# Gate and up products of a hierarchical mixture of experts: from fp32 to three fp32r products, with the weights split block by block on ScalarE and VectorE

## The reference

```
t = rms_norm(x, norm2_gain)
g_prob = softmax(t @ w_group + b_group); g = top 1 of g_prob
e_logit = t @ w_router + b_router;      2 best experts inside group g
gates = softmax(of the two logits) * p(g)
hg = einsum('td,edf->tef', t, w_gate)       # D = 1024, f = 256
hu = einsum('td,edf->tef', t, w_up)
a = silu(hg) * hu * gates
x = x + einsum('tef,efd->td', a, w_down)
```

## Time and profile before

| | |
|---|---|
| median of 3 runs | 1723.99 us (1722.34 to 1726.35) |
| the profiled execution, its own time | 1723.27 us |
| its span in the profile | 1721.4 us |
| PE busy | 1491.7 us (87%) |
| DVE busy | 781.1 us (45%) |
| ACT busy | 452.3 us (26%) |
| POOL busy | 315.3 us (18%) |
| DMA | 221.09 MB, mean 128 GB/s |

### The profile page before, as it was taken

How to read it: one execution, slowest core, us unless ns; L and a number is a source line. 1 busy time by engine, 2 the same in 40 slices (tenths; PEclk the granted TensorE clock), 3 DMA queues, 4 the chain that set the end, 5 groups by cost and what they waited for, 6 DMA issues and landing times.

```text
span 1721.4 us, 22556 instructions
## 1 busy us (share of the span) xinstructions
PE 1491.7 (87%) x6963; PEld 1079.8 (63%) x6964; DVE 781.1 (45%) x1883; ACT 452.3 (26%) x886; POOL 315.3 (18%) x204
## 2 busy tenths in 40 slices
PE   5999978998992999999289998899999749999990
PEld 4878867886882444444178786788778624444440
DVE  5777656663336122212267866656533452212210
ACT  4231245662111011111222222567412101111110
POOL 1000068001000122222500001930200012222224
PEclk9999989999995999999599999899999869999995
DMA  8000020000168499973870002000002945999947
GB/s 314 19 1 0 0 98 1 2 1 1 73 222 291 156 283 298 341 223 89 226 222 0 1 0 98 1 1 2 1 25 90 330 154 160 270 301 280 311 91 162
DMA packets 116624, 221.09 MB, mean 128 GB/s; under 512 B 5976, under 2 KB 72736, under 8 KB 116544
## 3 DMA queue, kind: packets, MB, share of 16 engines
q1 hardware_dynamic: 91744, 131.82, 22.2%
q0 software_dynamic: 19136, 69.38, 16.4%
q10 hardware_dynamic: 5664, 18.88, 2.8%
HBM read 170.77 MB, written 49.28 MB: 128 GB/s over the span
## 4 chain that ended last, share of the span: by engine, by line
PE 77%; DVE 7%; issue 6%; DMA 3%; ACT 2%; POOL 1%; ACTq 1%; DVEq 0%; PEld 0%; PEldq 0%; POOLq 0%; SPq 0%
PE ps L1566 19%; PE ps L1360 17%; PE ps L1340 11%; PE ps L1493 9%; PE ps L1579 9%; PE ps L1446 7%; PE ps L1420 2%; DMA out_x<-x_res,arena 2%; PE ps L1507 2%; PE ps L1422 1%; POOL out_x L622 1%; DVE arena L1149 1%; PE ps L1480 1%; DVE w_in_lo L944 1%; DMA big<-in_w_in 1%
## 5 line engine op out<-in xcount | busy, mean ns | idle before, releaser
L1566 PE MATMUL ps<-big,arena 128*128 x720 | 325.8, 606 | 9.6 <-issue 8.3
L1340 PE MATMUL ps<-cst,arena 128*128 128x128 f32 x1242 | 186.4, 284 | 76.4 <-DVE arena L915 37.6
L905 DVE TENSOR_TENSOR arena<-ps,par 128x512 f32<-128x512 f32 x126 | 81.2, 686 | 355.8 <-PE ps L1340 355.8
L1566 PEld LDWEIGHTS ps<-big,arena 128*128 128x128 f32 x720 | 135.7, 194 | 170.4 <-issue 170.4
L1340 PEld LDWEIGHTS ps<-cst,arena 128*128 128x128 f32 x1242 | 152.6, 146 | 122.7 <-DVE arena L915 39.3
L1360 PE MATMUL ps<-w_in_hi,hT_hi 128*128 128x512 f32 x512 | 206.1, 402 | 12.7 <-DVE hT_lo L933 9.9
L1360 PE MATMUL ps<-w_in_hi,hT_lo 128*128 128x512 f32 x512 | 202.1, 395 | 0.0
L1360 PE MATMUL ps<-w_in_lo,hT_hi 128*128 128x512 f32 x512 | 201.9, 394 | 0.0
L614 POOL DMA_INDIRECT x_res<-token_rows,row_tok x62 | 61.0, 985 | 605.1 <-issue 309.2
L1579 PE MATMUL ps<-big,arena 128*128 x360 | 163.8, 598 | 5.4 <-issue 5.4
L1446 PE MATMUL ps<-big,arena 128*128 128x64 f32 x1152 | 149.7, 278 | 0.0
(11 more groups left out here) (169 smaller groups left out, 1770.1 us busy)
## 6 DMA issues: line engine op xcount, KB each, us to landing
big<-in_w_gate SPq DMA_DIRECT2D x32, 1024.0 KB, 10.6
big<-in_w_up SPq DMA_DIRECT2D x32, 1024.0 KB, 13.1
big<-in_w_down SPq DMA_DIRECT2D x32, 1024.0 KB, 15.3
big<-in_w_in SPq DMA_DIRECT2D x16, 1024.0 KB, 9.5
big<-in_w_out SPq DMA_DIRECT2D x4, 2048.0 KB, 10.3
token_rows<-arena ACTq DMA_DIRECT2D x16, 512.0 KB, 3.3
out_x<-x_res ACTq DMA_DIRECT2D x16, 512.0 KB, 4.1
x_res<-out_x SPq DMA_DIRECT2D x8, 512.0 KB, 5.8
```

The source lines that it names most:

```text
L905: ins = ve.tensor_tensor(out=dst[:, 4 * h:4 * h + 4, :], in0=ps[:, banks + h, :].rearrange("p (a c) -> p a c", c=P), in1=spread(gain[:, 4 ...
L1340: ins = te.transpose(ps[:, bank + i // 4, (i % 4) * P:(i % 4 + 1) * P], src, ident)
L1566: ins = te.matmul(ps[:, 2, :], xgT[:, k, :], big[:, ds(at + k * 2 * FE, 2 * FE)], start=k == 0, stop=k == K - 1)
```

## The change

1. **Products.** `gate_up` takes 24 fp32r matmuls of 512 columns in place of 8 in fp32.
2. **Splitting the rows.** ACT copies the transposed rows of a block from PSUM into `xgT_hi` (`rows_high`, 128 x 1024) and DVE writes the rest into `xgT_lo` (`rows_evac`, 128 x 1024).
3. **Splitting the weights.** For every block, and again where two blocks share an expert, the gate and up weights are split in two halves of 128 x 2048: `gu_high` on ACT, `gu_low` on DVE. There are three buffers of a half, and half (t, h) goes to buffer (2t + h) mod 3. Each call looks up the block's expert in `block_e` with a register load from SBUF.
4. **Order.** In step t, ACT and DVE have, in this order:

```diff
+        xgT_hi = nc.alloc_sbuf_tensor_at("xgT_hi", [P, D], f32r, offset=xr_start)[:, :].rearrange("p (k n) -> p k n", n=P)
+        xgT_lo = nc.alloc_sbuf_tensor_at("xgT_lo", [P, D], f32r, offset=xr_start + 4 * D)[:, :].rearrange("p (k n) -> p k n", n=P)
+        HALF_GU = K * 2 * FE // 2
+        gu_hi = [part(f"gu_hi{i}", at, HALF_GU) for i, at in enumerate((0, 2 * HALF_GU, AT_A))]
+        gu_lo = [part(f"gu_lo{i}", at + HALF_GU, HALF_GU) for i, at in enumerate((0, 2 * HALF_GU, AT_A))]
...
+                def load_gu(e):
+                    slot = slot_of(e)
+                    for w, c in ((w_gate, 0), (w_up, K * FE)):
+                        sp.dma_start(w_gu[slot][:, c:c + K * FE],
+                                     w.rearrange("l e (p k) f -> p (l e) (k f)", k=K)[:, ds(l * NE + e, 1), :]
+                                     .rearrange("p a f -> p (a f)")).then_inc(s_gu[slot], 16)
...
+                for e in range(SLOTS, NE + 2):
+                    if e < NE:
+
+                        ended = sp.value_load(start_i[0:1, e - SLOTS + 1:e - SLOTS + 2], min_val=0, max_val=BLOCKS)
+                        sp.wait_ge(gu_split, upto(l, 2 * BLOCKS, 2 * ended))
+                        sp.sem_inc(s_passed, 1)
+                        load_gu(e)
+                    if SLOTS < e <= NE:
+                        report_gu(e - 1)
+                    d = e - 2
+                    if d >= SLOTS:
+                        ended = sp.value_load(start_i[0:1, d - SLOTS + 1:d - SLOTS + 2], min_val=0, max_val=BLOCKS)
                         sp.wait_ge(dn_done, upto(l, BLOCKS, ended))
...
+                        load_dn(d)
+                        if d > SLOTS:
+                            report_dn(d - 1)
...
-                in_high(l + 1, 0)
-
+                def gu_high(t, slot, h, half_of=None):
+
+                    e = a_.value_load(block_e[0:1, ds(t, 1)], min_val=0, max_val=NE - 1)
+                    if half_of is not None:
+                        a_.wait_ge(gu_half, upto(l, BLOCKS, half_of + 1))
+                        a_.sem_inc(s_passed, 1)
+                    a_.wait_ge(gu_loaded, upto(l, NE, e + 1))
+                    a_.sem_inc(s_passed, 1)
+                    at = ((e + 2) % SLOTS) * E_ALL + AT_E
+                    sc.activation(gu_hi[(2 * slot + h) % 3].rearrange("p (g c) -> p g c", g=2), raw_gu(at, h),
+                                  ACT.Copy).then_inc(gu_top, 1)
+
+                def rows_high(t):
+                    a_.wait_ge(xtm_done, upto(l, BLOCKS, t + 1))
+                    sc.activation(xgT_hi, ps[:, 0:2, :].rearrange("p a (k n) -> p (a k) n", n=P), ACT.Copy)\
+                        .then_inc(xg_top, 1)
...
                 def moe_act(t, slot, m):
+                    if not last(t, BLOCKS):
+                        gu_high(t + 1, (slot + 1) % RING, 1, t)
                     a_.wait_ge(gu_done, upto(l, BLOCKS, t + 1))
                     sc.activation(sg, ps[:, 2, 0:FE], ACT.Silu).then_inc(silu_done, 1)
+                    if not last(t, BLOCKS):
+                        a_.wait_ge(xgT_ready, upto(l, BLOCKS, t + 1))
+                        rows_high(t + 1)
+                    if not near_end(t, BLOCKS):
+                        gu_high(t + 2, (slot + 2) % RING, 0)
                     if not first(t):
                         moe_down(t - 1, *before(slot, m))
...
+                def gu_low(t, slot, h):
+
+                    dve.wait_ge(gu_top, upto(l, 2 * BLOCKS, 2 * t + h + 1))
+                    dve.sem_inc(s_passed, 1)
+                    e = dve.value_load(block_e[0:1, ds(t, 1)], min_val=0, max_val=NE - 1)
+                    at = ((e + 2) % SLOTS) * E_ALL + AT_E
+                    i = (2 * slot + h) % 3
+                    ve.tensor_tensor(out=gu_lo[i].rearrange("p (g c) -> p g c", g=2), in0=raw_gu(at, h),
+                                     in1=gu_hi[i].bitcast(f32).rearrange("p (g c) -> p g c", g=2), op=ALU.subtract).then_inc(gu_split, 1)
...
                 def moe_dve(t, slot, m):
                     if not last(t, BLOCKS):
-                        rows_evac(t + 1)
+                        gu_low(t + 1, (slot + 1) % RING, 1)
                     dve.wait_ge(silu_done, upto(l, BLOCKS, t + 1))
                     ve.scalar_tensor_tensor(out=act, in0=ps[:, 2, FE:2 * FE], scalar=list_gate[:, ds(t, 1)], in1=sg,
                                             op0=ALU.mult, op1=ALU.mult).then_inc(a_ready, 1)
+                    if not last(t, BLOCKS):
+                        rows_evac(t + 1)
+                    if not near_end(t, BLOCKS):
+                        gu_low(t + 2, (slot + 2) % RING, 0)
                     if not first(t):
                         y_evac(t - 1, *before(slot, m))
...
-                def gate_up(t):
-                    at = weights(t)
+                def gate_up(t, slot):
                     for k in range(K):
-                        ins = te.matmul(ps[:, 2, :], xgT[:, k, :], big[:, ds(at + k * 2 * FE, 2 * FE)],
-                                        start=k == 0, stop=k == K - 1)
+                        h = k // (K // 2)
+                        if k % (K // 2) == 0:
+                            pe.wait_ge(gu_split, upto(l, 2 * BLOCKS, 2 * t + h + 1))
+                        c = slice(k % (K // 2) * FE, (k % (K // 2) + 1) * FE)
+                        hi, lo = (w[(2 * slot + h) % 3].rearrange("p (g c) -> p g c", g=2)[:, :, c] for w in (gu_hi, gu_lo))
+                        for n, (a, b) in enumerate(((xgT_hi, hi), (xgT_hi, lo), (xgT_lo, hi))):
+                            ins = te.matmul(ps[:, 2, :].rearrange("p (g f) -> p g f", g=2), a[:, k, :], b, start=k == 0 and n == 0,
+                                            stop=k == K - 1 and n == 2)
+                        if k == K // 2 - 1:
+                            ins.then_inc(gu_half, 1)
                     ins.then_inc(gu_done, 1)
```

More of the change, by code:

```diff
@@ L866, in maybe_act @@
                         a_.sem_inc(aT_ready, 1)
+                        if not last(t, BLOCKS):
+                            a_.sem_inc(gu_top, 1 if near_end(t, BLOCKS) else 2)
+                            a_.sem_inc(xg_top, 1)
                 a_.wait_ge(routed, upto(l, 1, 1))
@@ L870, in _ @@
                 used = a_.value_load(start_i[0:1, NE:NE + 1], min_val=2 * SEQ // P, max_val=BLOCKS)
+                for h in range(2):
+                    gu_high(0, 0, h)
+                for i in range(2):
+                    a_.wait_ge(s_tok[i], (l + 1) * (16 * (T // 2)) + 1)
+                    a_.sem_inc(s_passed, 1)
+                a_.wait_ge(s_base, (l + 1) * (16 * T))
+                a_.sem_inc(s_passed, 1)
+                rows_high(0)
+                gu_high(1, 1, 0)
                 steps(a_, BLOCKS, moe_act, ring=RING, sure=SURE, maybe=maybe_act)
@@ L1595, in moe_pe @@
                     pe.sem_inc(s_passed, 1)
-                    gate_up(t)
+                    gate_up(t, slot)
+                    if first(t):
+                        list_gates()
                     if not last(t, BLOCKS):
```

151 lines of the change are left out of this document (95 added, 56 removed).

## The result

The changed kernel takes 1751.48 us (median of 4 runs, 1748.66 to 1758.33), the one before 1724.39 in the same session: ratio 1.0163, 95% interval 1.0128 to 1.0198. It was measured again beside the experiments: 1754.13, ratio 1.0177 (1.0118 to 1.0236). I had forecast 1717 and a range up to 1746: wrong in sign, and outside the range. The profiled execution took 1758.33 us, its span is 1756.4 (before 1721.4), so there are 35.0 us to find.

What follows compares the result with a forecast made beforehand. It took PE to bound the kernel before, and an ACT-DVE ring of 11.34 us a block after. Terms -9.2 + 5 + 2 + 2 - 2.5 - 4 = -6.7 on 1723.3 gave 1716.6, stated as 1717 us, range 1687 to 1746.

Steps and rivals of the forecast that it cites:

- PE's part: Expert blocks: 24 fp32r matmuls take 5.44 us in place of 6.87, so a PE-bound block would take 10.07 us.
- The ring: Expert blocks: ACT and DVE wait on each other in a once-a-block chain of 11.34 us, longer than PE's 10.07.
- The lookups cost more: Rival, expert blocks: slow register loads of 0.55 us or queue waits lengthen the chain to 11.8, +18 us, 1735; 30%.
- The steady part: Expert steps of both layers: 26 at 11.34 against 11.51 us, 13 at 11.54 against 11.91, together -9.2 us.
- The clock falls: Rival, expert blocks: PE's rests of 1.3 us a block bring stretches at half clock, +16 us, 1733; 5%.
- On the path for the last rows only: Out-projection: the extra instruction ahead of the gather and slower xs2 cost +1 us a layer (0.7 to 2), +2 together.
- The start of the stage: Expert stage behind the routing: first gate_up some 2.7 us late, +2.5 us a layer (0 to 5), +5 together.
- Between the layers -2.5: From layer 0 to layer 1: layer 1 starts 2.3 us later, but PE's 4.6 us third-tile wait goes; -5 to +3.
- the end of the layer: Last block of each layer: its aT stands behind two gu_low, +1 us each, +2 together.
- The tail: From the last used scatter to the end: without the unused gathers' bytes, -4 us (-6 to 0).
- Loads: Expert stage: lighter DMA but gate and up wanted earlier, 0 us (0 to +5); rival, late loads, 1730, 3%.
- DVE holds up the scatter: Rival, expert blocks: scatter lengthened beside DVE's gu_low, 12.2 us a block, some +33 us, 1750; 7%.

Runs made afterwards that it cites:

- experiments 1 and 8: 1: changed kernel, DVE's expert lookup ahead of its wait, 1706.93 us; 8: also contiguous xs2, x before weights, early silu table, y_evac first, 1679.58 us.
- experiment 2: Changed kernel with y_evac(t-1) ahead of gu_low(t+2, half 0) on DVE: 1719.66 us, ratio 0.9997.
- experiment 3: Changed kernel with one extra fp32 matmul filling PE's rest ahead of each gate_up: 1754.24 us, ratio 1.0196.
- experiment 11: Kernel of experiment 9 with gathers that skip nothing (unused rows at token 0, no bounds check): 1683.23 us, ratio 0.9765.
- experiment 9: Kernel of 8, but between layers input weights again ahead of x, their load waiting only for the last used block's y_evac: 1673.21 us, ratio 0.9716.
- single runs 5 and 6: 5: changed kernel, reload of x ahead of input weights between layers, 1767.68 us; 6: changed kernel, gathers without bounds check or skipped rows, 1777.47 us.

## Why the prediction was wrong

The forecast of 1716.6 for the profiled execution lies 41.7 us below the measured 1758.3. By the table of stages, 15.5 of them are in the steady steps, 11.7 in the out-projection, 6.8 at the end, 5.7 between the layers (with the end of layer 0) and 3.7 in the first stage, by chance; the start of the expert stage came out 1.9 us better than forecast.

- **PE's part: right.** 24 fp32r products follow each other by 0.227 us, and a step bound by PE is 10.01 us (I said 10.07).
- **The ring: right in order, and the bound,** as experiments 1 and 8 show, though experiment 2 found a second one right behind it that I had ruled out. In size, 11.28 against 11.34 is partly luck: the step shown has a load of 0.72, not 0.32. With a quick load the ring is 10.88 in the step shown and 11.12 in the mean; I had taken too much for the seams of the two queues.
- **"The lookups cost more": the rival that came, and the step of the forecast that cost most.** The seam ahead of `gu_low`, 1.2 with bounds of 0.8 and 1.7, was mis-sized: both rows that I had the earlier trace rows were taken while no scatter had been issued, and I took the larger for a bound. It went from 0.95 with a quick load to 2.1 (789.17 to 791.23). The steps with `If` became 12.6 and 12.2 in place of 11.54, and with PE's half clock the certain ones 11.46 and 11.61 in place of 11.34. The steady part was +6.3 us, not -9.2.
- **"The clock falls": came, at a small price.** Seven stretches in the steady steps, 2 to 5 us net in the traces and nothing in the times (experiment 3), against +16.
- **"On the path for the last rows only": the second step that failed,** and the one with the largest error for its size. I priced `xs2` between 0.7 and 2 us a layer, although my own upper bound for the instruction was 2.5. It is between the new x and PE's transposes in each of 8 row tiles. The out-projection lost 6.7 and 5.0 us; the term at the end of it (+1 a layer) was right, 1.2 and 1.0.
- **The start of the stage:** the first `gate_up` came 2.45 us later behind the routing (571.61 - 560.67 against 557.49 - 549.00; I said 2.7), and to the third silu it was +1.0 and +2.1 (+2.5). What I left out, silu's table load of 1.28 us behind the `gu_high`, PE's shorter products paid in part.
- **"Between the layers -2.5": wrong, with the end of the layer +4.2.** I costed the added waits of SP at nothing. `gu_split` for every block put the weights' load 10.5 us later, next to the reload of x, and ACT waited 4.29 us. PE's wait for the third rows went only from 4.6 to 2.65 us.
- **The tail:** skipping the gathers was worth 3.3 us (experiment 11; I said 4), but the last `aT` was 3.5 us later behind the silu, not 1, and the last `down` took 2.8 us longer at the lower clock.
- **Loads: right for the weights.** In the expert stages of the changed kernel and of experiments 8 and 9 no engine waits for an expert's weights, not even at steps of 10.0 us. What the full DMA engines do lengthen is the scatter's landing (experiment 9).
- **The scatter: right for this order.** It stayed at 1.59 us; only the gather met DVE. In the order of experiment 9 the rival "DVE holds up the scatter" does come, at 3.2 us a scatter.

The third rows of layer 1 come 70.7 us or more behind the last silu in every kernel, against 68.3 before, though SP could issue their reload at 59.1 in place of 61.2. They no longer wait for it: DVE comes to the same branch 5.8 us later (67.0 behind the last silu, 61.2 before), and behind it stand 3.2 us without a record (3.1 before, 5.3 in experiment 9). What stays open: what this time is; what a step of 10.3 to 11.9 us in experiments 8 and 9 owes to the scatter; and where the rest of the time of the single runs 5 and 6 went.

## What to carry to other kernels

Price a register load that an engine makes behind a wait as part of the chain, by its slow value, and put it ahead of the wait: it needs nothing that the wait gives, and here that one line decided between slower and faster than before. Where two rings have nearly the same length, shortening one gives only the difference; list every ring through a reused buffer with its length. For each wait that is added to a queue of transfers, look at what is issued behind it, and for an instruction that gets longer, count how many times it stands on the path before calling it hidden.

## What the runs showed of the hardware

- **A register load in the wake of a scatter.** In the changed kernel 74 of the 192 lookups on DVE and ACT begin 2.1 to 4.0 us behind the issue of a scatter; 42 of them took over 0.5 us, up to 1.3. Of the 118 others all but one (0.56, ahead of any scatter) took 0.33 or less. With `y_evac` first the slow ones lay at 2.5 to 5.4 us and reached 1.53. In experiment 9, where they stand ahead of the wait, none of DVE's loads was slow behind a scatter; 21 of ACT's were. That the scatter's traffic is the cause is argued from this, not shown by taking it away.
- **A gather beside `gu_low`** waits for it. Timeline of POOL in the step shown above, and of a gather that comes first:

```profile
617.03 2.82 POOL L665 DMA_INDIRECT x_res<-token_rows,row_tok  x1 [2.33 <-PE ps L1457]
...
661.81 1.04 POOL L665 DMA_INDIRECT x_res<-token_rows,row_tok  x1 [2.52 <-PE ps L1457]
```

  The first ends 0.9 us behind the `gu_low` of 616.66; the second began ahead of its `gu_low`. All 32 gathers of the changed kernel that start in a `gu_low` end 0.86 to 0.91 us behind it. The Trainium skill's page SBUF — State Buffer (section Who interferes with whom) says that a VectorE instruction with two SBUF inputs contends with a GpSimd instruction that reads SBUF, and infers that descriptor writing isn't held up; here the whole indirect gather was, and in experiment 9 the scatter.
